# Delta-rule heads in a two-block transformer kernel: another order of the same work on four engines

## What is computed

```
kb = kc * beta
lower = where(strict, (kb @ kc^T) * decay, 0)
u, w = solve(lower + I, [vc * beta, kb * exp(gc)])
for each chunk:
    v_new = u - w @ state
    out   = (q * exp(g)) @ state + (q @ k^T * decay) @ v_new
    state = state * exp(g_last) + (k * exp(g_last - g))^T @ v_new
```

## Time and profile before

| what | value |
|---|---|
| median of 3 runs | 2865.82 us (2862.32 to 2868.31) |
| the profiled execution | 2871.73 us, span 2869.6 us |
| busy share of the span | PE 94%, POOL 45%, DVE 40%, ACT 40% |
| mean granted TensorE clock | 0.974 |
| the four heads of layer 0 | 306 to 487 us |
| the four heads of layer 1 | 1023 to 1204 us |

### The profile page before, as it was taken

How to read it: one execution, slowest core, us unless ns; L and a number is a source line. 1 busy time by engine, 2 the same in 40 slices (tenths; PEclk the granted TensorE clock), 3 DMA queues, 4 the chain that set the end, 5 groups by cost and what they waited for, 6 DMA issues and landing times.

```text
span 2869.6 us, 37196 instructions
## 1 busy us (share of the span) xinstructions
PE 2706.4 (94%) x13032; PEld 2191.6 (76%) x13032; DVE 1152.9 (40%) x2171; ACT 1147.7 (40%) x1763; POOL 1305.2 (45%) x680
## 2 busy tenths in 40 slices
PE   7999889999999988999988799999999979999998
PEld 6768878887876887888877546888887855888887
DVE  3677543223567753322464544211102467221200
ACT  5437434323542743432453553333314455333321
POOL 4313564555631356455674211455546420465542
PEclk9999999999999999999998999999999989999999
DMA  4212101323321210033322100333333310233331
GB/s 171 83 45 67 42 26 30 95 96 112 94 83 37 67 44 24 30 95 97 123 87 75 38 29 27 92 96 95 101 95 112 102 45 1 88 95 95 100 97 66
DMA packets 61917, 215.07 MB, mean 75 GB/s; under 512 B 6864, under 2 KB 10064, under 8 KB 61392
## 3 DMA queue, kind: packets, MB, share of 16 engines
q1 hardware_dynamic: 61776, 213.27, 23.7%
HBM read 211.15 MB, written 2.10 MB: 74 GB/s over the span
## 4 chain that ended last, share of the span: by engine, by line
PE 81%; DVE 9%; POOL 4%; issue 3%; ACT 2%; DMA 0%; DVEq 0%; POOLq 0%; SPq 0%; ACTq 0%
PE bank L809 20%; PE bank L810 19%; PE bank L811 19%; PE pair L1501 3%; PE pair L809 2%; PE pair L811 2%; PE pair L810 2%; PE bank L1483 1%; PE bank L976 1%; PE bank L1462 1%; PE bank L1463 1%; DVE pair L2651 1%; DVE prod L2650 1%; POOL wl L2233 1%; DVE cpre L2665 1%
## 5 line engine op out<-in xcount | busy, mean ns | idle before, releaser
L2233 POOL TENSOR_TENSOR wl<-raw,wh 128x1024 fp32r<-128x1024 f32 x384 | 949.4, 2477 | 1425.7 <-ACT wh L1649 499.0
L809 PE MATMUL bank<-hh,wh 128*128 128x512 f32 x1536 | 608.3, 396 | 3.7 <-DVE y L2736 2.3
L810 PE MATMUL bank<-hl,wh 128*128 128x512 f32 x1536 | 599.7, 390 | 0.0
L811 PE MATMUL bank<-hh,wl 128*128 128x512 f32 x1536 | 599.5, 390 | 0.0
L809 PEld LDWEIGHTS bank<-hh,wh 128*128 128x128 f32 x1536 | 289.6, 189 | 66.8 <-issue 5.6
L810 PEld LDWEIGHTS bank<-hl,wh 128*128 128x128 f32 x1536 | 289.7, 189 | 61.6 <-issue 2.9
L811 PEld LDWEIGHTS bank<-hh,wl 128*128 128x128 f32 x1536 | 289.5, 188 | 61.0
L2185 ACT CAST wh<-raw 128x1024 fp32r<-128x1024 f32 x120 | 125.5, 1048 | 254.0 <-PE pair L811 140.2
L809 PE MATMUL bank<-wh,hh 128*128 128x512 f32 (+2 forms) x352 | 142.4, 405 | 19.6 <-POOL wl L2233 18.9
L810 PE MATMUL bank<-wl,hh 128*128 128x512 f32 (+2 forms) x352 | 137.1, 389 | 0.0
L811 PE MATMUL bank<-wh,hl 128*128 128x512 f32 (+2 forms) x352 | 136.9, 389 | 0.0
(11 more groups left out here) (461 smaller groups left out, 5403.6 us busy)
## 6 DMA issues: line engine op xcount, KB each, us to landing
raw<-stream SPq DMA_DIRECT2D x384, 512.0 KB, 3.6
mraw<-memin SPq DMA_DIRECT2D x3, 1024.0 KB, 5.6
par<-params SPq DMA_DIRECT2D x2, 1124.5 KB, 12.3
out<-xT SPq DMA_DIRECT2D x8, 256.0 KB, 2.8
con<-consts SPq DMA_DIRECT2D x1, 1540.0 KB, 16.3
xT<-xin SPq DMA_DIRECT2D x1, 1536.0 KB, 9.0
xT<-xin SPq DMA_DIRECT2D x1, 512.0 KB, 3.8
con<-consts SPq DMA_DIRECT2D x1, 512.0 KB, 3.1
```

The costliest lines, as they stand in the source:

```text
L809: mm(o, ah, bh, start=start, stop=False)
L810: mm(o, ah, bl, start=False, stop=False)
L811: return mm(o, al, bh, start=False, stop=stop)
L2233: return TT(wl[slot][:, :], raw[slot][:, :], wh[slot][:, :].bitcast(F32), ALU.subtract)
```

## The change

It moves work within the heads' programs; no instruction is added or taken away. On DVE the triangles of both directions come first, then both directions' `last` and `ST`; on ACT both `ET` come before both `EG`. The waits that named the old order are adapted (`e_ready`, and PE's first level waits for `lt_ready` instead of `st_ready`). On PE the new values of step 0 come ahead of the chunk products. On POOL `BV` comes before `KB`, `KDT` comes before the split `lo(40 + 2h)`, and `lo(41 + 2h)` goes behind the next head's placements (the last one stays at the end, as `lo(47)`). On ACT the Silu of gate `36 + 2h` and the cast of granule `40 + 2h` go between the copies of level 0 and those of level 1, and `WT` is copied behind step 0's `VN`.

```
@@ PE
-                                wait("e_ready", 2 * u + 2)
+                                wait("e_ready", 4 * h + 3 + d)
...
-                                wait("st_ready", 2 * h + 2)
+                                wait("lt_ready", 2 * h + 2)
...
-                    for d in range(2):
-                        u = 2 * h + d
-                        wait("rhs_ready", 6 * h + 2 * d + 1)
-                        wait("inv_ready", h * 6 + 5 + d)
-                        for c in range(NT):
-                            m = mm(b4[1 + d][:, c], KB[d][:, c], Y[d][:, c], start=True, stop=True)
-                        inc(m, "wt_done")
+                    def chunk_products():
+                        for d in range(2):
+                            wait("rhs_ready", 6 * h + d + 3)
+                            for c in range(NT):
+                                m = mm(b4[1 + d][:, c], KB[d][:, c], Y[d][:, c], start=True, stop=True)
+                            inc(m, "wt_done")
+                        wait("st_ready", 2 * h + 2)
...
                             if st == 0:
-                                wait("rhs_ready", 6 * h + 2 * d + 2)
+                                wait("rhs_ready", 6 * h + d + 1)
+                                wait("inv_ready", h * 6 + 5 + d)
                             mm_v = mm(b4[3 + d][:, c], Y[d][:, c], BV[d][:, c], start=True, stop=(st == 0))
...
+                        if st == 0:
+                            chunk_products()
@@ ACT
                         inc(A(ET[d]...), "e_ready")
+                    for d in range(2):
                         inc(A(EG[d]...), "e_ready")
                     for v in range(LEVELS):
                         for d in range(2):
                             wait("p1_done", h * 4 + 2 * v + d + 1)
                             inc(A(P1[d]...), "p1_ready")
-                    gate_z(2 * h, 7)
-                    hi(40 + 2 * h)
-                    for d in range(2):
-                        wait("wt_done", u + 1)
-                        inc(A(WT[d]...), "wt_ready")
+                        if v == 0:
+                            gate_z(2 * h, 7)
+                            hi(40 + 2 * h)
                     for st in range(NT):
+                        if st == 1:
+                            for d in range(2):
+                                wait("wt_done", 2 * h + d + 1)
+                                inc(A(WT[d]...), "wt_ready")
@@ POOL
                         inc(place(Y[d], d, 1 - d, h), "y0_ready")
+                    if h:
+                        lo(39 + 2 * h)
...
                     for d in range(2):
+                        wait("p1_done", h * 4 + 1 + d)
+                        inc(TT(BV[d]...), "rhs_ready")
+                    for d in range(2):
                         wait("p1_done", h * 4 + 3 + d)
                         inc(TT(KB[d]...), "rhs_ready")
-                        inc(TT(BV[d]...), "rhs_ready")
-                    lo(40 + 2 * h)
                     for d in range(2):
                         wait("a_done", h * 4 + 3 + d)
                         inc(TT(KDT[d]...), "rhs_ready")
-                    lo(41 + 2 * h)
+                    lo(40 + 2 * h)
+                lo(47)
@@ DVE
-                        wait("e_ready", 2 * u + 1)
+                        wait("e_ready", 4 * h + 1 + d)
                         inc(V.tensor_tensor(fl(P1), fl(ET), bk[3 + d], ALU.mult), "ub_ready")
                         wait("ub_ready", u + 1)
                         wait("kq_done", h + 1)
                         inc(V.tensor_tensor(fl(LT), fl(P1), bk[5], ALU.mult), "lt_ready")
-                        wait("e_ready", 2 * u + 2)
+                    for d in range(2):
+                        wait("e_ready", 4 * h + 3 + d)
                         step(V.tensor_copy(last[d][:, 0, :], EG[d][:, :, end]))
                         inc(V.tensor_copy(last[d][:, 1, :], ET[d][:, :, end]), "last_ready")
```

More of the change, by code:

```diff
@@ L1798, in _ @@
                             inc(A(P1[d][:, :, :].rearrange("p a b -> p (a b)"), bk[1 + d], ACT.Copy), "p1_ready")
-                    gate_z(2 * h, 7)
-                    hi(40 + 2 * h)
-                    for d in range(2):
-                        u = 2 * h + d
-                        wait("wt_done", u + 1)
-                        inc(A(WT[d][:, :, :].rearrange("p a b -> p (a b)"), bk[1 + d], ACT.Copy), "wt_ready")
+                        if v == 0:
+                            gate_z(2 * h, 7)
+                            hi(40 + 2 * h)
                     for st in range(NT):
+                        if st == 1:
+                            for d in range(2):
+                                wait("wt_done", 2 * h + d + 1)
+                                inc(A(WT[d][:, :, :].rearrange("p a b -> p (a b)"), bk[1 + d], ACT.Copy), "wt_ready")
                         for d in range(2):
@@ L2308, in _ @@
                         inc(TT(o, o, qT[h][:, :], ALU.mult), "qg_ready")
+                    b1 = [P, NT, P]
                     for d in range(2):
-                        u = 2 * h + d
-                        b1 = [P, NT, P]
+                        wait("p1_done", h * 4 + 1 + d)
+                        inc(TT(BV[d][:, :, :], vtok[h][:, :, :], bc(beta[:, :, d, h:h + 1], b1), ALU.mult), "rhs_ready")
+                    for d in range(2):
                         wait("p1_done", h * 4 + 3 + d)
                         inc(TT(KB[d][:, :, :], ktok[h][:, :, :], bc(nbeg[:, d, :, h:h + 1], b1), ALU.mult), "rhs_ready")
-                        inc(TT(BV[d][:, :, :], vtok[h][:, :, :], bc(beta[:, :, d, h:h + 1], b1), ALU.mult), "rhs_ready")
-                    lo(40 + 2 * h)
                     for d in range(2):
@@ L2697, in _ @@
                         u = 2 * h + d
-                        end = P - 1 if d == 0 else 0
                         fl = lambda t: t[d][:, :, :].rearrange("p a b -> p (a b)")
-                        wait("e_ready", 2 * u + 1)
+                        wait("e_ready", 4 * h + 1 + d)
                         inc(V.tensor_tensor(fl(P1), fl(ET), bk[3 + d], ALU.mult), "ub_ready")
@@ L2704, in _ @@
                         inc(V.tensor_tensor(fl(LT), fl(P1), bk[5], ALU.mult), "lt_ready")
-                        wait("e_ready", 2 * u + 2)
+                    for d in range(2):
+                        u = 2 * h + d
+                        end = P - 1 if d == 0 else 0
+                        wait("e_ready", 4 * h + 3 + d)
                         step(V.tensor_copy(last[d][:, 0, :], EG[d][:, :, end]))
```

## The result

The changed kernel takes 2826.6 us (median of 4 runs, 2820.06 to 2831.07) against 2867.07 us of the kernel before in the same measurement: a ratio of 0.985, with a 95% interval of 0.984 to 0.987, so 40.5 us. The forecast was 2819 us and 47 us.

The account below looks back on a forecast made before the run. PE bounds the kernel (81% of the chain), losing time to four holes and a clock fall per head. Gains of 4.7 + 1.25 = 5.95 us a head, 47 in eight, take the median from 2865.8 to 2819 us; range 2811 to 2831.

Parts of the forecast that it names:

- Triangles first: First level in each head: second direction's product starts at 364.0 instead of 365.75, gain 1.75 us.
- The levels: The two levels on PE keep their 8.28 us; the level-1 copy of P1 has 0.8 us of slack behind Silu and cast.
- New values first: Behind the levels: about 0.5 us new idle time before the second new value; the wait for VN closes.
- KDT ahead of the split: POOL before step 1: KDT ends at 376.4 with 0.35 us port wait, step 1 at 376.6; gain so far 4.7 us.
- The clock: PE in the heads: no long idle stretch remains, so the clock stays up, mean 1.00; gain 1.25 us a head.
- the gap of 1.39 us at 364.4 brought no fall: Argument against the clock falling all the same: PE's idle gap before the second direction's first level product left the clock up.
- The four steps: End of each head: step 1 takes 2.5 us instead of 3.76, and the head ends at 383.65 instead of 389.61.
- The sum over heads: All eight heads, reckoned from head 1: 5.95 us a head, 47 to 48 us in eight, 47 taken.
- With everything after the heads as it was, nothing is given back there: Code behind the heads: claimed to keep its timing, so no part of the heads' gain is lost there.
- The rival of the port in the heads: POOL as new bound: full 1.4 us of port waits, step 1 at 377.65, gain 39 us, 2827 us; chance 0.10.
- the one in which the clock falls all the same: Rival in the heads: remaining holes suffice, 1.25 us a head lost again, gain 37.6 us, 2828 us; chance 0.14.
- The rule that I set beside the sum: VectorE and GpSimd share a port; the second waits a whole instruction: 0.7 us before KDT, time about 3 us higher.

Follow-up runs that it names:

- e5: Changed kernel with the old order on DVE and ACT (each direction's triangle, copies and ST before the next; ET and EG in turn): 2850.92 us.
- e10: Kernel before with only both triangles first on DVE, both ET first on ACT and the waits that go with it: 2864.59 us, ratio 0.9986.
- e6: Changed kernel with the gate's Silu and the cast back behind the level-1 copies on ACT: 2828.06 us.
- e7: Changed kernel with the chunk products back ahead of the new values on PE and WT back ahead of VN on ACT: 2825.74 us.
- e9: Kernel before with only the two KDT products moved ahead of the split lo(40+2h) on POOL: 2838.39 us, ratio 0.990.
- e2: Changed kernel with the split lo(40+2h) back ahead of the two KDT products on POOL: 2853.11 us.
- e12: Kernel before, unedited, run again for a second profile: head 0 of layer 0 took 51.0 us at mean clock 0.83.
- e4: Kernel before with ACT writing the attention blocks' first square into the PSUM bank instead of SBUF: 2865.49 us, ratio 0.9985.
- e3: Changed kernel with ACT writing the attention blocks' first square into the PSUM bank instead of SBUF: 2820.18 us, ratio 0.982.

## Why the prediction was right

The mechanism, the place of each wait and the size of the gain in the heads were right: 44.9 us measured where 47 were forecast. Point by point, in the time of the kernel before:

- **Triangles first:** second product at 364.0, forecast; measured without any wait, the new values coming at 372.27 against 372.28. The part is worth more in company than I had it: undone alone it costs 33 us in the heads (`e5`), most of it by the clock; done alone it gains 0.4 us (`e10`), or 3.1 without the wait for the solver.
- **The levels:** unchanged length, and a slack of 0.69 us before the level-1 copy where I had 0.8.
- **New values first:** 0.5 us of new idle time was forecast, 0.31 measured. That no wait for `VN` is left is so. But of the two moves aimed at it, the one on ACT is worth nothing beside the other (`e6`), and the order on PE, together with the place of `WT`, 4.5 us (`e7`). I had booked no separate sum for either.
- **KDT ahead of the split:** end of the second KDT forecast at 376.4, measured at 376.45; the toll of the port was 0.34 us (2.49 against 2.15) where 0.35 was taken. This is the part that matters: 30 us alone (`e9`), 25 us in the heads when undone, without the wait for the solver (`e2`).
- **The clock:** forecast full, measured 1.00 in all eight heads. It fell at or behind the hole for KDT in the kernel before, in `e2` and in `e10`, and stayed full in `e9`, where only that hole was gone. But it isn't that hole alone: in `e5` and in head 0 of `e12` it fell behind the hole before the second level product, and in head 0 of `e4` all holes left it at 1.00. The prediction's reason "the gap of 1.39 us at 364.4 brought no fall" held for the one profile that I had; `e12` has a fall behind the same gap in head 0.
- **The four steps:** 2.50 us for step 1, as forecast. Step 1 starts at 376.82 instead of 376.6. The term that was mis-sized is the way from the end of KDT to step 1: I had allowed 0.2 us (376.4 to 376.6), and it took 0.37 (376.45 to 376.82), of which the product that waits for KDT takes 0.32 to the next start, where such pairs in a stream start 0.22 apart. With the 0.05 us of KDT itself that is 0.2 us a head, 1.8 us in eight.
- **The sum over heads:** heads 0 to 3 of layer 0 gain 5.8, 5.7, 5.6 and 5.4 us. Head 3 (45.88 to 40.47) had 0.14 us less idle time and 0.17 us less extra busy time to lose than head 1; the forecast took head 1 for all and never looked at head 3.

What failed is the sentence "With everything after the heads as it was, nothing is given back there". The code after the heads is the same and its timing is not: the race for DVE's and POOL's port in the second attention block cost 6.3 us in the profile, and the median with the edit of `e3` is 3.4 us lower, which is within the scatter of five runs. In the first measurement the gain is 6.5 us short of the forecast (40.5 against 47). The heads account for 2.1 of it; a long sum in most of its executions would account for the rest, but only the profiled one was seen.

The rival of the port in the heads (1.4 us) and the one in which the clock falls all the same are out by the rows above. The rule that I set beside the sum, from the Trainium skill, page "SBUF — State Buffer", section "SBUF: two separate sides", would have had 0.7 us in the heads by my reading, and the row there says 0.34. The row doesn't speak against the rule: DVE's product ended at 369.60 and POOL's pair began at 369.14, so less than a whole product lay in its way. In the attention block the trace agrees with it as far as it goes: a DVE product with two SBUF inputs waited behind whole POOL instructions, and with one input in PSUM (`e3`) it didn't wait at all. That it waited for three in a row is more than the rule states.

## What to carry to other kernels

Look for the work that stands in an in-order queue ahead of what the bounding engine waits for, and move that first: here two products ahead of a weight split that nobody wanted soon gave 30 us by itself, where all parts together gave 45. Price a hole in TensorE together with the clock behind it: a hole of 2.2 us cost 2.1 to 2.3 us where the clock held, 3.1 to 3.8 us where it fell behind KDT (`e2`) and 6.2 to 6.4 us where it fell in the level phase (`e5`), and a smaller hole elsewhere can leave the fall in place and gain nothing. Before calling the rest of a kernel unchanged, look for two engines that meet at a port within a microsecond or two: here the same DVE product took 1.6 us in some profiles and 8.6 in others.

## What was not expected of the hardware

- One DVE product of 128 x 512 took 8.56 us instead of 1.56, and ended 0.56 us behind three of POOL's splits, having waited through all of them; the kernel's copies in the heads (0.17 us alone) got in after one POOL product, at most 1.2 us. Putting one input in PSUM took the wait away.
- The same hole (2.17 us in `e5`, 2.15 us in `e2`) brought the clock from 2.4 GHz down in some heads of one execution and not in others, and the same head of unchanged code ran at a mean clock of 0.93, 0.83 and 1.00 in three profiles.
- With the holes the execution time also scatters: the kernel before ran from 2859.64 to 2877.83 us in 18 runs, one head 0 taking 46.1 and another 51.0 us. With the squares edit, so without the race, it still spread over 11.9 us in 12 runs (`e4`), while the changed kernel with that edit stayed within 3.1 us in 5 runs.
